# Sparse latent attention of a decoder layer: the second tile's logits in three fp32r passes, and the attention's output turned by VectorE alone

## The chip, the cores and the metric

One Trainium2 chip, one of its NeuronCores. The metric is the time of one execution on the device in microseconds. A core has TensorE (PE in the profile; PEld is its loading of stationary operands), VectorE (DVE), ScalarE (ACT), GpSimd (POOL) and SyncE (SP), which issues the DMAs here. The engines run their own lists of instructions and wait for each other on semaphores.

## The reference

One layer over 256 tokens of width 2048, in fp32. h = rmsnorm(x) is projected by one matrix; three token mixers read their columns; each mixer's output (256 x 1024) is gated by SiLU, projected to 2048 columns, scaled by a sigmoid gate and summed; one more projection, a norm and the residual follow. The mixer of the change is the third, cut to its core:

```python
def dsa_attention(q, ckv, iq, ik, iw, kv_norm_g, ik_norm_g, w_uv):
    q = q.reshape(b, s, 8, 256)                      # 8 heads, latent width 256
    c = rmsnorm(ckv, kv_norm_g)                      # 256 x 256, shared by the heads
    ...                                              # each query selects at most 64 keys
    logits = einsum('bqhc,bqkc->bqhk', q, c_sel) * 256 ** -0.5
    p = softmax(where(valid, logits, -inf))
    ob = einsum('bqhk,bqkc->bqhc', p, c_sel)
    return einsum('bqhc,hcv->bqhv', ob, w_uv)        # 8 heads x 128
...
y_c = dsa_attention(...) * silu(dsa_z)
mixed += sigmoid(gate_2) * (y_c @ w_branch[2])
```

## The kernel before

**Tiling.** The 256 tokens are two tiles of 128 partitions (TILES). All large products go through `multiply` (L1510): x (or y) is the stationary operand, split into a high part rounded to fp32r and the remainder (`xhi`/`xlo`, `yhi`/`ylo`); the weights are split the same way, and high x high, high x low and low x high are added in PSUM (L1526, L1527, L1528). Weights come in units of 256 rows by 512 columns (512 KB). For each unit SyncE loads `raw` (L392), ScalarE rounds it to `whi` (`round_unit`, L566), VectorE subtracts to `wlo` (`split_unit`, L894), and TensorE makes 12 matmuls of it, 2.72 us. The rings have 4 slots, and in step k the two engines prepare unit k + 4, once TensorE is through with unit k.

**Stages around the change.** Three loops follow each other, one for each mixer's output (parts PP[0], PP[1], PP[2], "branches" one to three). Each has 4 turns of 12 units: 8 units of the gate's projection (reads xhi, xlo), then 4 units of the branch's projection (reads yhi, ylo), and at the end of a turn VectorE gates the result and adds it to `mixed` (`gate_branch`, L1262: 4 instructions at L1268 and L1275). The order on each engine is written out by hand: the small work of the mixers is put between the units.

**Sparse attention** runs within the loop of PP[1]: two heads a turn, h = 2i + s, six steps (u) for each. `dsa_qT` holds q of one head turned, `cT` the latents turned; `chi` and `clo` are the split of `cT`, made earlier for another product.
- TensorE, u = 1: logits into M[1] (L1761 to 1765): columns 0:128 are tile 0 against keys 0:128, columns 128:384 tile 1 against all 256 keys, each as two fp32 matmuls over the latent width. u = 3: transposes of the probabilities (L1769). u = 4: times the values (L1777, L1779).
- VectorE, u = 1: mask (L1401) and maximum (L1404). u = 2: reciprocal of the sum and the SiLU gate (L1408 to 1411). u = 4: scale and gate the output into `area0` (L1418, `dsa_y`). u = 3 and 5: `turn_q` (L1323), 8 blocks each, turns q of the next head into `dsa_qT`; a block is one 32x32 STREAM_TRANSPOSE instruction over 128 elements (L885), and sixteen make a head.
- ScalarE, u = 2: exp (L809) and tanh for the gate (L813). u = 3: copies the transposes out (L817). Its loop over the turns is a hardware loop (L801).

**The output turned.** Branch three needs y turned and split in `yhi`/`ylo`, eight blocks of 128 columns in four pairs b. Before: pairs 0 and 1 (heads 0 to 3) are turned by VectorE with `turn_yc` (L1382), sixteen instructions of 32x256, four in each of the steps 0 to 3 of the first turn of PP[2], into `yc_T`; pairs 2 and 3 (heads 4 to 7) by eight transposes on TensorE after its first unit of that turn (L1806) into PSUM M[2] and M[3]. ScalarE rounds a pair with `round_y` (L787), VectorE subtracts with `split_y` (L1368). TensorE waits in `branch_units` (L1710) for the last `ylo` ahead of unit 8 of the turn. SyncE waits for the same `ylo` (L486) ahead of loading x again (1 MB), and the next turn's units are queued behind that.

Of the kernel before, what the change touches and what calls it, by code (L numbers as in the profile page):

```python
# [38 lines left out]
P = 128  # L39
D_MODEL = 2048  # L40
SEQ = 256
# [120 lines left out]
def build(nc, x, pre_norm_g, w_in, da_lambda, da_norm_g, ml_conv_w, ml_conv_b, ml_gate_b, ml_norm_g,  # L162
          dsa_kv_norm_g, dsa_ik_norm_g, dsa_w_uv, w_branch, w_out, post_norm_g, out):
    with ExitStack() as ctx:
# [17 lines left out]
        clo = sb("clo", [P, 2, SEQ], F32R)  # L182
        mixed = sb("mixed", [P, TILES, D_MODEL])
# [107 lines left out]
        yc_T = view(area0[:, 0, :], 2048, 4, SEQ)  # L291
# [68 lines left out]
        dsa_turned = sem("dsa_turned")  # L360
        dsa_logits, dsa_negmax, dsa_exp = sem("dsa_logits"), sem("dsa_negmax"), sem("dsa_exp")
# [3 lines left out]
        merged_turned, merged_psum, y_psum = sem("merged_turned"), sem("merged_psum"), sem("y_psum")  # L365
# [191 lines left out]
        def _(act):  # L557
# [243 lines left out]
            with act.Fori(0, PP[1].turns) as i:  # L801
                for v in range(PAIR_UNITS):
                    round_unit(PP[1], i, v)
                    s, u = v // 6, v % 6
                    h = i * 2 + s
                    if u == 2:
                        act.wait_ge(dsa_negmax, h * 2 + 2)
                        for t, a, n in ((0, 0, P), (1, P, 2 * P)):
                            nc.scalar.activation(dsa_s[:, a:a + n], dsa_s[:, a:a + n], ACT.Exp,  # L809
                                                 bias=dsa_negmax_c[:, t:t + 1], accum_out=dsa_sum_c[:, t:t + 1]  # L810
                                                 ).then_inc(dsa_exp, 1)
                        act.wait_ge(dsa_y, h * 2 + 1)
                        nc.scalar.activation(dsa_sig, area0[:, :, bass.ds(h * P + 3 * WIDTH, P)], ACT.Tanh,  # L813
                                             scale=0.5).then_inc(dsa_tz, 1)
# [17 lines left out]
            for i in range(PP[2].turns - 1):  # L832
                for v in range(PAIR_UNITS):
                    round_unit(PP[2], i, v)
                    if i == 0 and v == 0:
                        for b in range(2, 4):
                            act.wait_ge(y_psum, b - 1)
                            round_y(b, M[b][:, :].rearrange("p (k s) -> p k s", k=2))
                    if i == 0 and v == 4:
                        for b in range(2):  # L840
                            act.wait_ge(y_turned, 4 + b + 1)
                            round_y(b, yc_T[:, 2 * b:2 * b + 2, :])
                    if v == FULL_UNITS - 1:
                        gates(PP[2], i, 8)
# [34 lines left out]
        def _(dve):  # L879
# [501 lines left out]

            def turn_yc(n):  # L1382

                if n == 0:
                    dve.wait_ge(dsa_y, 1 + TILES * DSA_HEADS // 2)
                last = turn_block(yc_T.rearrange("p k (t s) -> p k t s", t=TILES),
                                  area0[:, :, 3 * WIDTH:3 * WIDTH + 512].rearrange("p t (k d) -> p k t d", d=P), n)
                if n == 15:
                    last.then_inc(y_turned, 2)

            for i in range(PP[1].turns):
                steps.enter(0, 2 * 4)
                for v in range(PAIR_UNITS):
# [3 lines left out]
                    if u in (3, 5) and h < DSA_HEADS - 1:  # L1397
                        turn_q(h + 1, range(8) if u == 3 else range(8, 16))
# [15 lines left out]
                    if u == 4:  # L1414

                        dve.wait_ge(dsa_out, h + 1)
                        for t in range(TILES):
                            nc.vector.scalar_tensor_tensor(area0[:, t, bass.ds(h * P + 3 * WIDTH, P)],  # L1418
                                                           M[3][:, t * P:(t + 1) * P], dsa_rsum_c[:, t:t + 1],
                                                           dsa_sig[:, t, :], ALU.mult, ALU.mult).then_inc(dsa_y, 1)  # L1420
                gate_branch(PP[1], i, 4)
# [13 lines left out]
            for i in range(PP[2].turns - 1):  # L1435
                for v in range(PAIR_UNITS):
                    split_unit(PP[2], i, v)
                    if i == 0 and v < 4:
                        for n in range(4):
                            turn_yc(4 * v + n)  # L1440
                    if i == 0 and v == 1:
                        for b in range(2, 4):
                            split_y(b, M[b][:, :].rearrange("p (k s) -> p k s", k=2), 8 + b - 1)
                    if i == 0 and v == 5:
                        for b in range(2):
                            split_y(b, yc_T[:, 2 * b:2 * b + 2, :], 10 + b + 1)
# [62 lines left out]
        def _(pe):  # L1509
# [240 lines left out]
            with pe.Fori(0, PP[1].turns) as i:  # L1750
                for v in range(PAIR_UNITS):
# [6 lines left out]
                    if u == 1:  # L1758
                        pe.wait_ge(ylo_ready, 9)
                        pe.wait_ge(dsa_turned, h + 1)  # L1760
                        for t, a, n in ((0, 0, P), (1, P, 2 * P)):  # L1761
                            for c in range(2):
                                last = nc.tensor.matmul(M[1][:, a:a + n], dsa_qT[:, c, t * P:(t + 1) * P],  # L1763
                                                        cT[:, c, 0:n], start=(c == 0), stop=(c == 1))
# [28 lines left out]
            def pair_turn(i, first):  # L1793

                for v in range(PAIR_UNITS):
# [4 lines left out]
                    if first and v == 0:  # L1800
                        pe.wait_ge(dsa_y, 1 + TILES * DSA_HEADS)
                        for b in range(2, 4):
                            for j in range(2):
                                for t in range(TILES):
                                    kt = 2 * b + j
                                    last = nc.tensor.transpose(M[b][:, j * SEQ + t * P:j * SEQ + (t + 1) * P],  # L1806
                                                               area0[:, t, 3 * WIDTH + kt * P:3 * WIDTH + (kt + 1) * P],
                                                               ident[:, :])
                            last.then_inc(y_psum, 1)

            pair_turn(0, True)
            with pe.Fori(1, PP[2].turns - 1) as i:
                pair_turn(i, False)
# [52 lines left out]
```

## Time and profile before

| | before |
|---|---|
| median of 3 runs | 1093.58 us (1093.2 to 1093.67) |
| profiled execution, its time | 1092.95 us |
| its span, first to last instruction | 1091.2 us |
| TensorE busy | 1080.8 us |
| VectorE busy | 810.7 us |
| ScalarE busy | 538.7 us |
| GpSimd busy | 15.0 us |
| mean granted TensorE clock | 0.998 |

How to read it: "busy" is the time in which at least one instruction of the engine was running. Matmuls overlap, a matmul of 512 columns is shown with some 0.39 us but one starts every 0.227 us, so prices on TensorE are read from starts. The time of an execution is 1.75 us more than its span here. In the timelines below a line is the start, the duration, the engine, the source line, the operation, output and input, shapes, the number of instructions merged, and in brackets the idle time of the engine before it with what ended it.

### The profile page before, as it was taken

To read this page: it belongs to the slowest core of one execution; us is meant where nothing else is said; L and a number is where in the kernel's file an instruction comes from. 1 tells how busy PE (TensorE), PEld (TensorE's weight loads), DVE (VectorE), ACT (ScalarE), POOL (GpSimd) and SP (SyncE) were. 2 spreads that over 40 slices of the span, in tenths; PEclk is the share of its full clock that TensorE was granted. 3 is DMA by queue.
4 is the path that set the end of the run, shared out by engine and by line. 5 is a ranking of instruction groups with operands and counts; after the bars stand their busy time and mean duration, and the time that the engine had idled before them with its cause. 6 is when DMAs were issued, how large, how long until landed. Compare 5 with 4: busy or idle time off the path is not lost.

```text
span 1091.2 us, 14577 instructions
## 1 busy us (share of the span) xinstructions
PE 1080.8 (99%) x5041; PEld 896.6 (82%) x5041; DVE 810.7 (74%) x1441; ACT 538.7 (49%) x751; POOL 15.0 (1%) x41
## 2 busy tenths in 40 slices
PE   9999999999999999999999999999999999999997
PEld 7898888888887888889887778888888888888886
DVE  5555566688877888888888777878788777777445
ACT  5664444555555565555446444454444444436442
POOL 0000000000000000000000000000000000000000
PEclk9999999999999999999999999999999999999999
DMA  8776666566656656657656555654655567765552
GB/s 283 200 220 193 193 193 193 175 186 177 192 174 176 181 163 190 196 160 229 207 161 190 175 170 174 213 175 141 196 171 163 153 219 259 229 196 182 194 194 109
DMA packets 114122, 205.83 MB, mean 189 GB/s; under 512 B 11229, under 2 KB 18457, under 8 KB 113689
## 3 DMA queue, kind: packets, MB, share of 16 engines
q1 hardware_dynamic: 114032, 205.21, 61.8%
q8 instruction: 25, 0.41, 0.1%
q14 instruction: 25, 0.20, 0.1%
q10 hardware_dynamic: 40, 0.01, 0.0%
HBM read 203.10 MB, written 2.10 MB: 188 GB/s over the span
## 4 chain that ended last, share of the span: by engine, by line
PE 92%; DVE 6%; ACT 1%; issue 0%; DMA 0%; DVEq 0%; ACTq 0%
PE stream L1526 29%; PE stream L1528 28%; PE stream L1527 28%; DVE wlo L894 2%; PE stream L1647 1%; PE mixer L1763 1%; DVE mixed L885 1%; DVE area L885 1%; ACT whi L566 1%; PE stream L1648 0%; PE mixer L1779 0%; PE mixer L1625 0%; PE mixer L1730 0%; PE mixer L1561 0%; PE mixer L1729 0%
## 5 line engine op out<-in xcount | busy, mean ns | idle before, releaser
L566 ACT ACTIVATE whi<-raw 128x1024 fp32r<-128x1024 f32 (+1 forms) x376 | 395.5, 1054 | 505.6 <-PE stream L1528 479.2
L894 DVE TENSOR_TENSOR wlo<-raw,whi 128x1024 fp32r<-128x1024 f32 (+1 forms) x376 | 456.4, 1217 | 243.0 <-ACT whi L566 239.6
L1526 PE MATMUL stream<-whi,xboth 128*128 128x512 f32 (+1 forms) x1248 | 490.4, 393 | 0.0
L1528 PE MATMUL stream<-whi,xboth 128*128 128x512 f32 (+1 forms) x1248 | 484.0, 388 | 0.0
L1527 PE MATMUL stream<-wlo,xboth 128*128 128x512 f32 (+1 forms) x1248 | 483.6, 387 | 0.0
L1526 PEld LDWEIGHTS stream<-whi,xboth 128*128 128x128 f32 x1248 | 234.5, 188 | 50.9 <-issue 4.9
L1528 PEld LDWEIGHTS stream<-whi,xboth 128*128 128x128 f32 x1248 | 234.4, 188 | 48.5
L1527 PEld LDWEIGHTS stream<-wlo,xboth 128*128 128x128 f32 x1248 | 234.6, 188 | 46.0
L1526 PE MATMUL stream<-whi,yhi 128*128 128x512 f32 x192 | 76.7, 399 | 0.3 <-DVE ylo L1368 0.3
L1528 PE MATMUL stream<-whi,ylo 128*128 128x512 f32 x192 | 75.0, 390 | 0.0
L1527 PE MATMUL stream<-wlo,yhi 128*128 128x512 f32 x192 | 74.8, 389 | 0.0
L885 DVE STREAM_TRANSPOSE mixed<-area 32x128 f32<-32x128 f32 x224 | 67.7, 302 | 3.7
L885 DVE STREAM_TRANSPOSE scratch<-area 32x128 f32<-32x128 f32 (+1 forms) x160 | 50.5, 316 | 2.8
L1526 PEld LDWEIGHTS stream<-whi,yhi 128*128 128x128 f32 x192 | 36.1, 188 | 8.4 <-issue 1.3
L1528 PEld LDWEIGHTS stream<-whi,ylo 128*128 128x128 f32 x192 | 36.0, 188 | 7.8
L1527 PEld LDWEIGHTS stream<-wlo,yhi 128*128 128x128 f32 x192 | 36.1, 188 | 7.3
L1647 PE MATMUL stream<-xboth,whi 128*128 128x384 f32 x120 | 35.1, 361 | 0.2 <-ACT area L573 0.2
L1648 PE MATMUL stream<-xboth,wlo 128*128 128x192 f32 x120 | 30.0, 250 | 0.0
L573 ACT ACTIVATE area<-stream,tiny 128x512 f32<-128x512 f32 (+1 forms) x44 | 27.6, 677 | 3.3 <-DVE mixed L885 2.9
L1647 PEld LDWEIGHTS stream<-xboth,whi 128*128 128x128 f32 x120 | 22.6, 188 | 0.6 <-issue 0.4
L1648 PEld LDWEIGHTS stream<-xboth,wlo 128*128 128x128 f32 x120 | 22.9, 191 | 0.1
L885 DVE STREAM_TRANSPOSE area<-mixed 32x256 f32<-32x256 f32 x48 | 20.9, 436 | 1.0
(241 smaller groups left out, 554.1 us busy)
## 6 DMA issues: line engine op xcount, KB each, us to landing
raw<-in_w_in SPq DMA_DIRECT2D x286, 512.0 KB, 3.6
raw<-in_w_branch SPq DMA_DIRECT2D x48, 512.0 KB, 4.6
raw<-in_w_out SPq DMA_DIRECT2D x32, 512.0 KB, 3.7
raw<-in_w_in SPq DMA_DIRECT2D x12, 256.0 KB, 3.2
mixed<-in_x SPq DMA_DIRECT2D x8, 256.0 KB, 6.5
area<-in_x SPq DMA_DIRECT2D x2, 1024.0 KB, 6.6
out<-area SPq DMA_DIRECT2D x8, 256.0 KB, 2.3
raw<-in_dsa_w_uv SPq DMA_DIRECT2D x4, 256.0 KB, 2.9
```

What stands on the lines that cost most here:

```text
L566: nc.scalar.activation(whi[:, slot, :, 0:width], raw[:, slot, :, 0:width], ACT.Copy).then_inc(whi_ready, 1)
L573: nc.scalar.activation(to[t], stream[bank_pair][t][:, 0:width], ACT.Copy, scale=rstdx[:, t:t + 1]).then_inc(banks_free, 1)
L885: return nc.vector.transpose(to[c * 32:(c + 1) * 32, :, :, p * 32:(p + 1) * 32], of[p * 32:(p + 1) * 32, :, :, c * 32:(c + 1) * 32])
L894: nc.vector.tensor_tensor(wlo[:, slot, :, 0:width], raw[:, slot, :, 0:width], whi[:, slot, :, 0:width].bitcast(F32), ALU.subtract).then_in ...
L1526: nc.tensor.matmul(to, left_hi[:, kt, tokens], high, start=first, stop=False)
L1527: nc.tensor.matmul(to, left_hi[:, kt, tokens], low, start=False, stop=False)
L1528: last = nc.tensor.matmul(to, left_lo[:, kt, tokens], high, start=False, stop=final)
L1647: nc.tensor.matmul(both_to, high, xboth[:, kt, :, TOPK:], start=kt == 0, stop=False)
L1648: last = nc.tensor.matmul(low_to, low, xhi[:, kt, TOPK:], start=False, stop=False)
L1763: last = nc.tensor.matmul(M[1][:, a:a + n], dsa_qT[:, c, t * P:(t + 1) * P], cT[:, c, 0:n], start=(c == 0), stop=(c == 1))
```

## The change

The part of tile 1 of the logits is computed in three fp32r passes. ScalarE rounds the turned q of tile 1 to `dsa_qhi`, VectorE makes the remainder `dsa_qlo` (`split_q`), and TensorE adds qhi x chi, qhi x clo and qlo x chi over both halves of the latent width, six matmuls of 256 columns in place of two fp32 ones. Tile 0 stays as it is. TensorE waits for `dsa_qlo` between the two. ScalarE's copy for the next head stands in its step u = 5 behind the rounding, and waits for the turned q; VectorE's subtraction in its step u = 5. The turns of q move from steps 3 and 5 (8 and 8) to steps 2, 3 and 4 (4, 6 and 6). ScalarE's loop over the turns is written out in the program.

The output is turned by VectorE alone. Heads 0 to 3 are turned (sixteen 32x256 instructions) in steps 1 to 5 of the last head (2, 3, 4, 3, 4), heads 4 to 7 in steps 0 to 3 of branch three's first turn, four each. The eight transposes on TensorE go, and its first turn of branch three joins the loop. `round_y` stands in steps 0 (pairs 0, 1) and 4 (pairs 2, 3), `split_y` in steps 1 and 5.

```diff
@@ -288,7 +290,7 @@
-        yc_T = view(area0[:, 0, :], 2048, 4, SEQ)
+        yc_T = [view(area0[:, c, :], 2048, 4, SEQ) for c in range(2)]
@@ -798,11 +801,18 @@
-            with act.Fori(0, PP[1].turns) as i:
+            act.wait_ge(dsa_turned, 1)
+            nc.scalar.activation(dsa_qhi[:, :, :], dsa_qT[:, :, P:], ACT.Copy).then_inc(dsa_qhi_ready, 1)
+
+            for i in range(PP[1].turns):
                 for v in range(PAIR_UNITS):
                     round_unit(PP[1], i, v)
                     s, u = v // 6, v % 6
                     h = i * 2 + s
+                    if u == 5 and h < DSA_HEADS - 1:
+                        act.wait_ge(dsa_logits, h + 1)
+                        act.wait_ge(dsa_turned, h + 2)
+                        nc.scalar.activation(dsa_qhi[:, :, :], dsa_qT[:, :, P:], ACT.Copy).then_inc(dsa_qhi_ready, 1)
@@ -832,14 +842,10 @@
-                    if i == 0 and v == 0:
-                        for b in range(2, 4):
-                            act.wait_ge(y_psum, b - 1)
-                            round_y(b, M[b][:, :].rearrange("p (k s) -> p k s", k=2))
-                    if i == 0 and v == 4:
-                        for b in range(2):
+                    if i == 0 and v in (0, 4):
+                        for b in range(v // 2, v // 2 + 2):
                             act.wait_ge(y_turned, 4 + b + 1)
-                            round_y(b, yc_T[:, 2 * b:2 * b + 2, :])
+                            round_y(b, yc_T[b // 2][:, 2 * (b % 2):2 * (b % 2) + 2, :])
@@ -1379,13 +1385,23 @@
+            def split_q(h):
+
+                dve.wait_ge(dsa_qhi_ready, h + 1)
+                nc.vector.tensor_tensor(dsa_qlo[:, :, :], dsa_qT[:, :, P:], dsa_qhi[:, :, :].bitcast(F32),
+                                        ALU.subtract).then_inc(dsa_qlo_ready, 1)
+
+            split_q(0)
+
             def turn_yc(n):
 
-                if n == 0:
-                    dve.wait_ge(dsa_y, 1 + TILES * DSA_HEADS // 2)
-                last = turn_block(yc_T.rearrange("p k (t s) -> p k t s", t=TILES),
-                                  area0[:, :, 3 * WIDTH:3 * WIDTH + 512].rearrange("p t (k d) -> p k t d", d=P), n)
-                if n == 15:
+                c = n // 16
+                if n % 16 == 0:
+                    dve.wait_ge(dsa_y, 1 + TILES * DSA_HEADS // 2 * (c + 1))
+                last = turn_block(yc_T[c].rearrange("p k (t s) -> p k t s", t=TILES),
+                                  area0[:, :, 3 * WIDTH + c * 512:3 * WIDTH + (c + 1) * 512].rearrange(
+                                      "p t (k d) -> p k t d", d=P), n % 16)
+                if n % 16 == 15:
                     last.then_inc(y_turned, 2)
@@ -1394,8 +1410,8 @@
-                    if u in (3, 5) and h < DSA_HEADS - 1:
-                        turn_q(h + 1, range(8) if u == 3 else range(8, 16))
+                    if u == 5 and h < DSA_HEADS - 1:
+                        split_q(h + 1)
@@ -1418,6 +1434,11 @@
+                    if u in (2, 3, 4) and h < DSA_HEADS - 1:
+                        turn_q(h + 1, {2: range(4), 3: range(4, 10), 4: range(10, 16)}[u])
+                    if 0 < u and h == DSA_HEADS - 1:
+                        for n in {1: range(2), 2: range(2, 5), 3: range(5, 9), 4: range(9, 12), 5: range(12, 16)}[u]:
+                            turn_yc(n)
@@ -1437,13 +1458,10 @@
                     if i == 0 and v < 4:
                         for n in range(4):
-                            turn_yc(4 * v + n)
-                    if i == 0 and v == 1:
-                        for b in range(2, 4):
-                            split_y(b, M[b][:, :].rearrange("p (k s) -> p k s", k=2), 8 + b - 1)
-                    if i == 0 and v == 5:
-                        for b in range(2):
-                            split_y(b, yc_T[:, 2 * b:2 * b + 2, :], 10 + b + 1)
+                            turn_yc(16 + 4 * v + n)
+                    if i == 0 and v in (1, 5):
+                        for b in range(v // 2, v // 2 + 2):
+                            split_y(b, yc_T[b // 2][:, 2 * (b % 2):2 * (b % 2) + 2, :], 8 + b + 1)
@@ -1758,10 +1776,15 @@
-                        for t, a, n in ((0, 0, P), (1, P, 2 * P)):
-                            for c in range(2):
-                                last = nc.tensor.matmul(M[1][:, a:a + n], dsa_qT[:, c, t * P:(t + 1) * P],
-                                                        cT[:, c, 0:n], start=(c == 0), stop=(c == 1))
+                        for c in range(2):
+                            nc.tensor.matmul(M[1][:, 0:P], dsa_qT[:, c, 0:P], cT[:, c, 0:P],
+                                             start=(c == 0), stop=(c == 1))
+                        pe.wait_ge(dsa_qlo_ready, h + 1)
+                        for c in range(2):
+                            to = M[1][:, P:3 * P]
+                            nc.tensor.matmul(to, dsa_qhi[:, c, :], chi[:, c, :], start=(c == 0), stop=False)
+                            nc.tensor.matmul(to, dsa_qhi[:, c, :], clo[:, c, :], start=False, stop=False)
+                            last = nc.tensor.matmul(to, dsa_qlo[:, c, :], chi[:, c, :], start=False, stop=(c == 1))
                         last.then_inc(dsa_logits, 1)
@@ -1790,27 +1813,16 @@
-            def pair_turn(i, first):
+            def pair_turn(i):
...
-                    if first and v == 0:
-                        pe.wait_ge(dsa_y, 1 + TILES * DSA_HEADS)
-                        for b in range(2, 4):
-                            for j in range(2):
-                                for t in range(TILES):
...
-                            last.then_inc(y_psum, 1)
...
-            pair_turn(0, True)
-            with pe.Fori(1, PP[2].turns - 1) as i:
-                pair_turn(i, False)
+
+            with pe.Fori(0, PP[2].turns - 1) as i:
+                pair_turn(i)
```

## Rows read from the trace of the kernel before

**Rows 1.** The page, part 1: busy time, share of the span, instructions.

```profile
PE 1080.8 (99%) x5041; PEld 896.6 (82%) x5041; DVE 810.7 (74%) x1441; ACT 538.7 (49%) x751; POOL 15.0 (1%) x41
```

**Rows 2.** Waits, 712 to 900 us: waiter, what it waited for, total, times, longest.

```profile
PE stream L1526 <- DVE ylo L1368: 0.3, 1, 0.3
```

**Rows 3.** The chain that ended last, 845 to 905 us: start, duration, engine, line.

```profile
850.64 1.31 PE mixer L1763 x8
...
864.02 1.07 ACT whi L566
...
866.26 1.28 DVE area L1268 x2
...
868.77 1.23 DVE wlo L894
...
881.62 0.45 DVE area L885
...
882.63 0.62 ACT yhi L787
...
884.23 1.23 DVE wlo L894
885.46 1.21 DVE ylo L1368 x2
...
886.91 0.47 PE stream L1526
```

**Rows 4.** Timeline of TensorE around the logits of head 1.

```profile
737.84 1.47 PE L1763 MATMUL mixer<-scratch 128*128 128x128 f32 x8
...
739.38 0.40 PE L1527 MATMUL stream<-wlo,yhi 128*128 128x512 f32 x1
```

**Rows 5.** Timeline of TensorE: the small projection, then the indexer's queries.

```profile
58.79 0.32 PE L1526 MATMUL stream<-whi,xboth 128*128 128x344 f32 x1
...
68.91 0.32 PE L1526 MATMUL stream<-whi,xboth 128*128 128x344 f32 x1
...
500.91 0.25 PE L1648 MATMUL stream<-xboth,wlo 128*128 128x192 f32 x1
...
501.20 0.25 PE L1648 MATMUL stream<-xboth,wlo 128*128 128x192 f32 x1
```

**Rows 6.** Timeline of VectorE: head 7, then the first turns of the output.

```profile
855.85 1.23 DVE L894 TENSOR_TENSOR wlo<-raw,whi 128x1024 fp32r<-128x1024 f32 x1 [1.74 <-ACT whi L566]
...
857.39 0.43 DVE L1411 SCALAR_TENSOR_TENSOR scratch<-scratch,area 128x256 f32<-128x256 f32 x1
858.65 1.23 DVE L894 TENSOR_TENSOR wlo<-raw,whi 128x1024 fp32r<-128x1024 f32 x1 [0.83 <-ACT whi L566]
861.67 1.23 DVE L894 TENSOR_TENSOR wlo<-raw,whi 128x1024 fp32r<-128x1024 f32 x1 [1.80 <-ACT whi L566]
...
865.11 1.23 DVE L894 TENSOR_TENSOR wlo<-raw,whi 128x1024 fp32r<-128x1024 f32 x1 [1.70 <-ACT whi L566]
...
869.92 1.77 DVE L885 STREAM_TRANSPOSE area<-area 32x256 f32<-32x256 f32 x4
```

**Rows 7.** Timeline of VectorE: head 0, a group of turns of q and the output's scaling.

```profile
728.39 2.50 DVE L885 STREAM_TRANSPOSE scratch<-area 32x128 f32<-32x128 f32 x8
...
732.05 0.60 DVE L1418 SCALAR_TENSOR_TENSOR area<-mixer,tiny,scratch 128x128 f32<-128x128 f32 x2
```

**Rows 8.** Timeline of TensorE: the output's transposes and the second matmul behind them.

```profile
866.55 1.04 PE L1806 MATMUL mixer<-ident,area 128*128 128x128 f32 x8
...
867.66 0.39 PE L1527 MATMUL stream<-wlo,xboth 128*128 128x512 f32 x1
```

**Rows 9.** Stretches at the end: stretch, length, busy (count) of PE, PEld, DVE, ACT, POOL; clock; DMA share, GB/s.

```profile
1084.00:1085.00 1.00, 0.20 (x1) 0.00 (x0) 0.05 (x1) 0.69 (x2) 0.00 (x0) 1.00 0.72 275
...
1087.00:1088.00 1.00, 0.00 (x0) 0.00 (x0) 1.00 (x3) 0.00 (x0) 0.00 (x0) 0.71 0.64 240
```

## Prediction: what the change does to the time

> **What bounds the kernel now.** I read four views in this order. First the page: TensorE is busy for 99% of the span and VectorE for 74% [rows 1], so the time is TensorE's list of work plus whatever it waits for. Then the waits of the stretch that the change touches (712 to 900 us): TensorE waits for another engine there once, 0.3 us, for `ylo` of L1368 [rows 2]. Then the chain that ended last, between 845 and 905 us. The reader is to see in it where it leaves TensorE: up to the rounding at 864.02 it is TensorE's stream, then it runs over VectorE (L1268 at 866.26, the split of unit 0 at 868.77, the turns of the output, the last at 881.62), ScalarE (`yhi`, 882.63), VectorE again (split of unit 5 at 884.23, `ylo` at 885.46), and TensorE's first product with y starts at 886.91 [rows 3]. So VectorE has no slack between about 866 and 887 us although it is idle a quarter of the whole time: the wait of 0.3 us is what is left of a race that TensorE nearly ties. What TensorE saves before 855 us shortens the kernel; what it saves between 866 and 887 us only lengthens that wait; what VectorE gets extra ahead of 882 us lengthens the kernel. Last, the timelines of TensorE and VectorE price the parts.
>
> **Logits of the second tile (L1761 to 1765), eight times.** The block of one head is eight records: each fp32 product is two records. It takes 1.31 us in the chain [rows 3]; in the timeline it begins at 737.84 and the stream's pitch is regained with the matmul at 739.38 [rows 4], (739.38 - 737.84) less one pitch of 0.227 = 1.31 again. Four records have 128 columns, four 256: by columns 1.31/12 = 0.109 for a short one, 0.218 for a long one. The short ones stay (0.44). The long ones (0.87) give way to six fp32r products of 256 columns. None of that width is in the trace. From the small projection, 344 columns: from 58.79 to 68.91 are 66 matmuls, 0.153 each [rows 5]; with 0.227 for 512 that is 0.44 ns a column, so 0.115 us at 256. The other bound is a pair of 384 and 192 columns, 501.20 - 500.91 = 0.29 for 576 columns [rows 5], 0.127 us at 256. I take 0.116, since equal passes in a row are like the small projection: 6 x 0.116 = 0.70. Saving per head 0.87 - 0.70 = 0.17 (bounds 0.11 and 0.18), times eight 1.4 us (0.9 to 1.5; if the additional wait in the middle of the block stops the look-ahead of the weights, it can fall to nothing, a rival below). It is all on the path, as all eight blocks come before 855 us, where the chain is TensorE's.
>
> The Trainium skill (TensorE: Matmul & The Clock Gate, Back-to-back issue gap) gives an isolated gap of the columns at 2.4 GHz plus some 2.5 ns. Here the 512 columns take 227 ns, some 11 ns more than that rule gives. By the rule a pass would be 0.109 and the eight heads would save 1.7 us, 0.3 more than my sum; the rows decide.
>
> **Feeding these products.** New per head: a copy to `dsa_qhi` on ScalarE (128x256, 0.4 us by the nearest row of that shape, L1411 of VectorE at 0.43 [rows 6]) and a subtraction on VectorE (same shape, 0.4). The wait for `dsa_turned` stands in ScalarE ahead of the next unit's rounding, the wait for `dsa_qhi` in VectorE ahead of the next split. The turns of q are spread anew: eight 32x128 turns take 2.50 us, 0.31 each [rows 7]; they now are 4, 6 and 6 in steps 2, 3 and 4, where they were 8 and 8 in steps 3 and 5. L1418 of head 0 is at 732.05 and takes 0.60 [rows 7]; it comes no later than now, as 10 turns and not 8 stand ahead but four of them in the idle time before step 3. Then six turns to 734.5; the split of step 5 (1.25) to 735.8, and the subtraction to 736.2. TensorE's next block starts at 737.84 [rows 4]: 1.6 us to spare, so these cost nothing. ScalarE's copy at 734.5 lies between the roundings. Once the cover of 1.6 us is gone each microsecond more costs one per head. Before the loop the pair for head 0 fits in the same way; ScalarE's loop written out turn by turn, and TensorE's first turn of branch three folded into the loop, I put at nothing: neither engine's issue is late in this stretch (ScalarE waits there for TensorE, the only wait of TensorE is the one above).
>
> **Eight transposes less on TensorE (L1806).** They begin at 866.55, and the pitch is regained at 867.66 [rows 8]: 1.11 less 0.23 is 0.88 us. That lies after 866 us, where VectorE is the chain. So TensorE comes 0.88 us earlier to the wait for `ylo` and waits 0.88 longer: worth nothing. That is the main difference between the work saved and the time saved.
>
> **Sixteen turns more on VectorE, in the last head.** Four turns of 32x256 in branch three take 1.77 with a pitch of 1.79 to the next [rows 6], 0.447 each. The change puts sixteen of them, 7.15 us, into steps 1 to 5 of head 7 (2, 3, 4, 3, 4). Head 7 has no turns of q in either kernel, so they fall into idle time first: 1.74 before the split at 855.85, 0.83 before 858.65, then 1.80 and 1.70 [rows 6]. I follow the engine. Step 1: two turns end by 855.0, before the split of step 2 can start: free. Step 2: split at 855.85, L1411 at 857.39 to 857.85, three turns to 859.19. Step 3: split 1.25, four turns 1.80, to 862.24. Step 4: split 1.15, L1418 0.62, three turns 1.34, to 865.35. Step 5: split 1.25, four turns 1.80, to 868.40. The gating (L1268, L1275) takes 868.77 - 866.26 = 2.51 [rows 3], to 870.91. Before, the next split started at 868.77 [rows 3]. So VectorE enters branch three 2.14 us late, with no idle time left in which to catch up: the four steps with turns (c = 1) and the two `ylo` of the first half in step 1 are the same work as now. The 32 turns thus end at 884.2, not 882.06, and the tail from there (ScalarE's `yhi`, the rounding of unit 5, VectorE's split and two `ylo`) takes the same 4.8 us: TensorE's product with y starts at 889.05 on the clock of before. The extra 2.14 (bounds 1.8 and 2.6: a split takes 1.23 [rows 6] and lets its follower start after 1.15 to 1.25, the first of the turns after 869.92 - 868.77 = 1.15 [rows 3, 6]) is on the path in full. No unit is late meanwhile: the closest is unit 8's split, done 885.4 where TensorE wants it at 885.6.
>
> **After the wait** everything is tied to `ylo` in both kernels: ScalarE's next roundings, the DMA queue (x again and the next turn's units are queued behind the same wait), and VectorE's next splits. So the shift stays as it is to the end.
>
> **Sum.** -1.4 (logits) + 2.14 (turns) + 0 (transposes) = +0.75 us. The profiled execution took 1092.95 (span 1091.2), which would become 1093.7 (span 1092.0). The median of the runs shown is 1093.58, 0.63 above it: 1094.3.
>
> **Rivals.**
> (1) The clock falls in the gap. TensorE's idle time before its first product with y grows from 0.28 to 0.28 + 0.88 + 2.14 = 3.3 us. At the end of the span TensorE's last work ends at 1084.2, and the granted clock is down in the stretch from 1087 on, 0.71 in that microsecond, which puts the fall at 1087.4, 3.2 us after the last matmul [rows 9]. The gap is as long as that, a coin's throw against its phase; against it speaks that there the idleness had no end. Each microsecond at the low level (1.2 GHz) loses half a microsecond. How soon it rises again no row shows; taken as the 3.2 us that it took to fall, 1.6 us is lost, up to 3 if it takes twice that: 1095.9 (to 1097.3). This ends on the slow side, and decides from a gap of about 3 us. The skill (same page, HAM oscillation — how this bites in real kernels) says that a TensorE left without work in gaps is put back to the low clock and has to earn the high one anew; the trace agrees for its one long gap, the end, and this rule speaks against the change.
> (2) The three passes save nothing, as the additional wait in the middle keeps the next weights from being loaded ahead, or they run at the price of 0.145 each: +2.14, 1095.7. For it: six instructions of 0.12 us in place of four of 0.22; against it: the waits that stand ahead of such blocks now show no gap [rows 4].
> (3) The turns are hidden after all, because some of VectorE's idle time that I count as used stays: then the wait for `ylo` doesn't grow but goes. -1.4 - 0.88 - 0.28 = -2.6, 1091.0. Against it: the chain runs over VectorE there now [rows 3], and 7.15 us go into about 5 that can be used.
> (4) The subtraction for `dsa_qlo` comes later than 1.6 us more than worked out, and TensorE waits in each head; at 0.5 us a head +4 on top: 1098.
>
> **How the numbers follow.** Forecast 0.60, (1) 0.18, (2) 0.10, (3) 0.08, (4) 0.04. Most likely 1094.3. The range takes in the forecast with its bounds (0.9 to 1.5 saved, 1.8 to 2.6 added: 1093.9 to 1095.3, and half a microsecond for the median), (2) and most of (1): 1092.6 to 1096.9. 0.2%, about what a measurement of this kernel can tell from no change, is 2.2 us. Faster is (3), 0.08. Slower is most of (1), part of (2) and (4), 0.22. Within is the rest, 0.70.
>
> **What would show it.** Right: L1763's successor at some 1.14 us a block; TensorE's wait for `ylo` 3.2 to 3.5 us and still its only one in the stretch; no VectorE idle time from 856 to 884; the gating of head 7's turn 2.1 us later against TensorE's stream. Wrong: a wait for `dsa_qlo`; a granted clock under 1.00 near 890 us; a wait for `ylo` under 1 us.

## The result

The changed kernel took 1095.08 us (median of 15 executions, 1093.79 to 1097.03), the kernel before 1093.24 (15 executions, 1092.55 to 1093.67): ratio 1.0023, 95% interval 1.0016 to 1.0030. That is 1.84 us more by the medians, whose own ratio is 1.0017 and lies within the interval. The forecast was 1094.3 within 1092.6 to 1096.9.

The executions of the changed kernel don't lie around one value. Each has a mean granted clock of its span: three have 0.998, as in the profiled execution of before, and took 1093.79, 1093.97 and 1094.34; six have 0.996 or 0.997 and took 1094.83 to 1095.09; six have 0.995 and took 1096.53 to 1097.03. The profiled one is of the last kind (1096.83, span 1095.1).

The waits from 712 to 900 us, where before there was only [rows 2] for TensorE (waiter, what it waited for: total, times, longest):

```profile
ACT dsa_qhi L815 <- DVE scratch L891: 6.7, 7, 1.0
PE stream L1544 <- DVE ylo L1374: 3.4, 1, 3.4
```

ScalarE waits for the turned q at most 1.0 us a head, which stays hidden. TensorE still waits for another engine once, for `ylo`, but 3.4 us and not 0.3. No wait for `dsa_qlo` has appeared. The timeline of VectorE from head 7 on answers to [rows 6]:

```profile
854.93 1.23 DVE L900 TENSOR_TENSOR wlo<-raw,whi 128x1024 fp32r<-128x1024 f32 x1 [0.78 <-ACT whi L569]
...
858.27 1.22 DVE L900 TENSOR_TENSOR wlo<-raw,whi 128x1024 fp32r<-128x1024 f32 x1
...
861.32 1.22 DVE L900 TENSOR_TENSOR wlo<-raw,whi 128x1024 fp32r<-128x1024 f32 x1
...
864.45 1.23 DVE L900 TENSOR_TENSOR wlo<-raw,whi 128x1024 fp32r<-128x1024 f32 x1
865.70 1.80 DVE L891 STREAM_TRANSPOSE area<-area 32x256 f32<-32x256 f32 x4
867.53 1.29 DVE L1274 SCALAR_TENSOR_TENSOR area<-area,stream 128x512 f32<-128x512 f32 x2
...
870.05 1.22 DVE L900 TENSOR_TENSOR wlo<-raw,whi 128x1024 fp32r<-128x1024 f32 x1
...
883.37 1.22 DVE L900 TENSOR_TENSOR wlo<-raw,whi 128x1024 fp32r<-128x1024 f32 x1
885.50 1.22 DVE L900 TENSOR_TENSOR wlo<-raw,whi 128x1024 fp32r<-128x1024 f32 x1 [0.91 <-ACT whi L569]
886.65 1.28 DVE L1374 TENSOR_TENSOR ylo<-area,yhi 128x512 fp32r<-128x512 f32 x2
```

After the split at 854.93 the brackets are gone: the idle times of 0.83, 1.80 and 1.70 us in [rows 6] are filled, and VectorE works without a break to 884.6. TensorE at the wait and behind it:

```profile
884.36 0.39 PE L1546 MATMUL stream<-whi,xboth 128*128 128x512 f32 x1
888.17 0.79 PE L1544 MATMUL stream<-whi,yhi 128*128 128x512 f32 x1 [3.43 <-DVE ylo L1374]
...
889.19 0.63 PE L1546 MATMUL stream<-whi,ylo 128*128 128x512 f32 x1
889.62 0.63 PE L1544 MATMUL stream<-whi,yhi 128*128 128x512 f32 x1
...
893.82 0.40 PE L1545 MATMUL stream<-wlo,yhi 128*128 128x512 f32 x1
894.06 0.39 PE L1546 MATMUL stream<-whi,ylo 128*128 128x512 f32 x1
```

Two things are to be seen. The product with y starts after 3.43 us without work, and then a matmul starts every 0.43 us and not every 0.23, until 893.5. The stretches say why (start and end, length, busy time and count of PE, PEld, DVE, ACT, POOL, granted clock, DMA share, GB/s):

```profile
884.00:886.00 2.00, 0.74 (x4) 0.28 (x2) 1.09 (x2) 2.00 (x4) 0.00 (x0) 1.00 0.18 70
886.00:888.00 2.00, 0.00 (x0) 0.00 (x0) 2.00 (x4) 2.00 (x4) 0.00 (x0) 0.73 0.00 0
888.00:890.00 2.00, 1.82 (x4) 1.49 (x5) 2.00 (x2) 0.52 (x1) 0.00 (x0) 0.50 0.41 82
890.00:892.00 2.00, 2.00 (x6) 1.57 (x5) 0.20 (x1) 0.00 (x0) 0.00 (x0) 0.50 0.97 399
892.00:894.00 2.00, 2.00 (x6) 1.57 (x6) 0.00 (x0) 0.00 (x0) 0.00 (x0) 0.57 1.00 384
894.00:896.00 2.00, 2.00 (x10) 1.63 (x10) 0.54 (x1) 1.06 (x1) 0.00 (x0) 1.00 1.04 399
```

The granted clock falls to 0.50 (1.2 GHz) within the idle stretch, at about 886.9 us, and is back at 2.4 GHz at about 893.7. From 888.17 to there are 5.6 us at the low level. What they cost is seen in the rest of the span, which is the same work in both kernels: from the first product with y to the last instruction there are 1091.2 - 886.91 = 304.3 us before and 1095.1 - 888.17 = 306.9 changed, so 2.6 us are lost. The Trainium skill (TensorE: Matmul & The Clock Gate, HAM oscillation — how this bites in real kernels) tells of a TensorE that waits in gaps between its work, is put back to the low clock and starts again at it. This trace agrees, with these rows.

**Where the time went.** The spans differ by 3.9 us. To separate the parts I take the time from the first block of logits, before which the two programs differ in nothing that takes time on TensorE, to the first product with y. It leaves out the 0.5 us by which executions differ at the very start. The first block starts here in the kernel before and in the changed one (timelines of TensorE):

```profile
719.08 1.47 PE L1763 MATMUL mixer<-scratch 128*128 128x128 f32 x8
```

```profile
719.55 0.60 PE L1780 MATMUL mixer<-scratch 128*128 128x128 f32 x4
719.91 0.36 PE L1785 MATMUL mixer<-chi,dsa_qhi 128*128 128x256 f32 x1
720.11 0.28 PE L1786 MATMUL mixer<-clo,dsa_qhi 128*128 128x256 f32 x1
720.23 0.28 PE L1787 MATMUL mixer<-chi,dsa_qlo 128*128 128x256 f32 x1
...
720.70 0.40 PE L1544 MATMUL stream<-whi,xboth 128*128 128x512 f32 x1
720.94 0.40 PE L1545 MATMUL stream<-wlo,xboth 128*128 128x512 f32 x1
```

Before, the product with y starts at 886.91 [rows 3], 167.83 us after 719.08. Changed, it is 888.17 - 719.55 = 168.62: 0.79 us more, where the sum of the prediction says 0.75. The rest of the 3.9 us is the start (0.47) and the low clock (2.6): 0.79 + 0.47 + 2.6 = 3.9.

### The profile page after: what moved, and what is told of

It is laid out like the page before. It is cut to its first block, busy times and chain, and to the rows that moved or that the text cites. A ratio compares the mean times of both kernels' runs of the same rounds, so it can differ in the third digit from the quotient of the medians.

```text
span 1095.1 us, 14580 instructions
## 1 busy us (share of the span) xinstructions
PE 1081.4 (99%) x5049; PEld 897.5 (82%) x5049; DVE 820.8 (75%) x1465; ACT 541.4 (49%) x759; POOL 15.0 (1%) x41
## 4 chain that ended last, share of the span: by engine, by line
PE 91%; DVE 7%; ACT 1%; issue 1%; DMA 0%; DVEq 0%; ACTq 0%
PE stream L1544 29%; PE stream L1546 28%; PE stream L1545 28%; DVE wlo L900 3%; DVE area L891 1%; PE stream L1665 1%; DVE mixed L891 1%; ACT whi L569 1%; PE stream L1666 0%; PE mixer L1643 0%; PE mixer L1780 0%; PE mixer L1748 0%; PE mixer L1579 0%; PE mixer L1747 0%; PE mixer L1802 0%
## 5 line engine op out<-in xcount | busy, mean ns | idle before, releaser
L891 DVE STREAM_TRANSPOSE area<-area 32x256 f32<-32x256 f32 x48 | 20.9, 436 | 1.0
```

Source lines behind the costliest of these rows:

```text
L891: return nc.vector.transpose(to[c * 32:(c + 1) * 32, :, :, p * 32:(p + 1) * 32], of[p * 32:(p + 1) * 32, :, :, c * 32:(c + 1) * 32])
```

## The experiments

In the table "way" is the time from the first block of logits to the first product with y, from the profiled execution of each kernel; "wait" is TensorE's wait for `ylo` there; the ratio is to the kernel before on the same chip.

| kernel | way, us | wait, us | median, us | ratio, 95% interval |
|---|---|---|---|---|
| before | 167.83 | 0.28 | 1093.24 | |
| changed | 168.62 | 3.43 | 1095.08 | 1.0023 (1.0016 to 1.0030) |
| logits_only | 166.42 | 0.30 | 1091.22 | 0.9986 (0.9977 to 0.9995) |
| turns_only | 169.98 | 3.37 | 1097.04 | 1.0038 (1.0025 to 1.0052) |
| before_late2 | 169.99 | 2.42 | 1096.80 | 1.0033 (1.0022 to 1.0043) |
| warm20 | 168.67 | 1.28 | 1093.88 | 1.0007 (0.9998 to 1.0016) |
| warm10 | 168.66 | 2.37 | 1094.07 | 1.0012 (1.0003 to 1.0021) |
| first_half_early | 165.96 | none | 1090.54 | 0.9982 (0.9973 to 0.9991) |
| spread | 166.64 | 1.22 | 1091.57 | 0.9989 (0.9980 to 0.9998) |
| spread_ylo4 | 165.29 | none | 1090.45 | 0.9978 (0.9969 to 0.9987) |

**One part alone: the logits.** The changed kernel, with the output's part put back:

```diff
-                    if 0 < u and h == DSA_HEADS - 1:
-                        for n in {1: range(2), 2: range(2, 5), 3: range(5, 9), 4: range(9, 12), 5: range(12, 16)}[u]:
-                            turn_yc(n)
...
-                            turn_yc(16 + 4 * v + n)
+                            turn_yc(4 * v + n)
...
+                    if first and v == 0:
+                        pe.wait_ge(dsa_y, 1 + TILES * DSA_HEADS)
...
```

> The kernel before with the logits' part of the change alone (three passes, the split of q, the turns of q moved); the output is turned as before. Theory (the eight shorter blocks are on the path, as they lie ahead of the stretch where VectorE is the chain): 1.4 us less than before, 1091.8 against 1093.2; TensorE's wait for ylo stays at about 0.3 us, no clock under 1.00 near 890 us. Rival (the six passes with the additional wait cost as much as the four long records): no change, 1093.2.

The way is 1.41 us shorter, the wait stays at 0.30, the clock at 1.00. The median is 1.95 less than that of before on its chip (1093.17), with an interval of 0.5 to 2.5 that holds the 1.4. The three passes bring what they were said to, and that part alone makes the kernel faster.

**The other part alone: the output.** The kernel before with the output's part of the change, logits as they were:

```diff
-                        for c in range(2):
-                            nc.tensor.matmul(M[1][:, 0:P], dsa_qT[:, c, 0:P], cT[:, c, 0:P],
-                                             start=(c == 0), stop=(c == 1))
-                        pe.wait_ge(dsa_qlo_ready, h + 1)
...
+                        for t, a, n in ((0, 0, P), (1, P, 2 * P)):
+                            for c in range(2):
...
```

> The kernel before with the output's part alone (all turns on VectorE, sixteen in head 7); logits as before. Theory: VectorE enters branch three 2.1 us late, TensorE's product with y starts 2.1 us later and its wait grows to 3.3 us: 1095.4 where the clock holds, and up to 2.5 us more (1097.9) in runs in which it falls in that gap, so several levels of time within one kernel. Rival (the two parts only cost when together, since the split of q on VectorE makes the lateness): under 1094.

The way is 2.15 us longer, the wait 3.37. So the two parts add: -1.41 + 2.15 = +0.74, against +0.79 for both. The lateness of VectorE is due to the turns and not to the split of q. The median is up by 3.87, more than 2.15, and the profiled execution shows the rest; these are its matmuls after the wait:

```profile
889.25 0.49 PE L1534 MATMUL stream<-whi,yhi 128*128 128x512 f32 x1 [3.37 <-DVE ylo L1367]
889.58 0.49 PE L1535 MATMUL stream<-wlo,yhi 128*128 128x512 f32 x1
889.87 0.63 PE L1536 MATMUL stream<-whi,ylo 128*128 128x512 f32 x1
890.30 0.63 PE L1534 MATMUL stream<-whi,yhi 128*128 128x512 f32 x1
...
892.86 0.53 PE L1534 MATMUL stream<-whi,yhi 128*128 128x512 f32 x1
893.23 0.39 PE L1535 MATMUL stream<-wlo,yhi 128*128 128x512 f32 x1
```

Here the clock falls when TensorE has already been at work again for half a microsecond (0.43 us from start to start only from 889.87 on; the granted clock of the stretch from 888 to 890 is 0.93, which puts the fall at 889.7). In the stretch from 892 to 894 it is 0.71, so it is back at 893.2: low for 3.4 us, which costs 1.7 (from the first product with y to the end there are 306.0 us in place of 304.3), and 2.15 + 1.7 = 3.85. The 1095.4 that was expected where the clock holds can't be seen: all five executions have a mean clock of 0.995 to 0.997.

**Fill the gap.** The changed kernel, with 20 (then 10) transposes of the identity on TensorE between its last work ahead of the wait and the wait:

```diff
+                    if first and v == FULL_UNITS - 1:
+                        for _ in range(20):
+                            nc.tensor.transpose(M[2][:, 0:P], ident[:, :], ident[:, :])
```

> The changed kernel with 20 transposes of the identity on TensorE (0.11 us each, 2.1 us) into a free bank right ahead of the wait for ylo in branch three's first turn: they fill the gap, and leave about 1.3 us of it. Theory (the spread of the changed kernel's times, 1093.8 to 1097.0, is the clock falling in the gap): the clock stays at 1.00 there, all runs lie within 1093.3 to 1094.4, median 1094.0, although TensorE does more. Rival (the spread comes from the loads queued behind the same wait): levels and median stay as they are, 1095.1, or rise by the work added.

TensorE does 2 us more work and the kernel is 1.2 us faster than the changed one (1.1 us, where each is compared with the kernel before on its own chip: +0.71 and +1.84). The way is the same (168.67 against 168.62), as the wait shrinks by what the transposes take. The spread is gone: eleven executions within 1093.31 to 1094.46, against 1093.79 to 1097.03. So the difference between the forecast's 0.75 and the measured 1.84 us, and the levels, are the clock's.

> The changed kernel with 10 transposes of the identity in the gap ahead of the wait for ylo, half of what warm20 had: some 2.3 us of the gap are left. Theory (only the length of TensorE's idle stretch and its phase decide whether the clock falls, as in before_late2, where 2.4 us was enough in most runs): some runs fall and some don't, two levels about 1.7 us apart, 1093.8 and 1095.5. Rival (what matters is that TensorE was idle for over 3 us, and the levels of before_late2 come from something else): one level as with warm20, 1093.9.

The theory's first half came out and its distance did not. Eight executions have a mean clock of 0.998 and took 1093.87 to 1094.42; three have 0.996 or 0.997 and took 1094.87 to 1095.00, some 0.9 us more and not 1.7. So the single level of the rival is not there. Why the three lose only 0.9 us stays open, as none of them was profiled. The profiled execution is one of the eight and keeps its clock over a gap of 2.37 us:

```profile
886.00:888.40 2.40, 0.03 (x2) 0.04 (x1) 2.40 (x4) 2.40 (x4) 0.00 (x0) 1.00 0.01 3
888.40:892.00 3.60, 3.60 (x16) 3.00 (x17) 2.01 (x2) 0.31 (x1) 0.00 (x0) 1.00 0.77 257
```

So a gap of 2.4 us keeps the clock in most executions of this kernel and loses it in some. The next kernel has a gap of the same length and loses it in most. The length by itself doesn't settle it.

**The lateness by itself.** The kernel before, with seven additional turns on VectorE:

```diff
+                    if i == 0 and v in (2, 3):
+                        for n in range(4 if v == 2 else 3):
+                            turn_block(view(area1[:, 1, :], 3 * WIDTH, 4, SEQ).rearrange("p k (t s) -> p k t s", t=TILES),
+                                       area0[:, :, 3 * WIDTH:3 * WIDTH + 512].rearrange("p t (k d) -> p k t d", d=P),
+                                       4 * v + n)
```

> The kernel before with seven additional 32x256 turns on VectorE in steps 2 and 3 of branch three's first turn, written to an area that nobody reads (3.1 us more on VectorE, none of the change). Theory: it passes one to one to TensorE's product with y, the wait for ylo grows from 0.3 to 3.4 us and the kernel by 3.1 us, 1096.3 where the clock holds and up to 2.5 more where it falls. Rival (VectorE has slack there, and the changed kernel's lateness comes from elsewhere): less than 1.5 us more, under 1094.8.

The way grows by 2.16 us and not by 3.1, the wait to 2.42. The timeline of VectorE shows where the remainder went:

```profile
877.52 3.57 DVE L885 STREAM_TRANSPOSE area<-area 32x256 f32<-32x256 f32 x8
881.10 1.23 DVE L894 TENSOR_TENSOR wlo<-raw,whi 128x1024 fp32r<-128x1024 f32 x1
882.36 3.17 DVE L885 STREAM_TRANSPOSE area<-area 32x256 f32<-32x256 f32 x7
885.54 2.36 DVE L894 TENSOR_TENSOR wlo<-raw,whi 128x1024 fp32r<-128x1024 f32 x2
887.82 1.29 DVE L1368 TENSOR_TENSOR ylo<-area,yhi 128x512 fp32r<-128x512 f32 x2
```

I had put the last three behind the real turns, whose last releases ScalarE. ScalarE rounds meanwhile, and VectorE's splits of units 8 and 9 now stand without the pause of 0.9 us between them that it otherwise spends waiting for ScalarE. Four of the seven (1.79) pass in full, the other three (1.34) less that 0.9: 2.2, as measured. The theory's one to one holds only ahead of the last turn. The kernel does nothing of the change, but it has the gap, and its times lie in two groups, 1094.34 and 1094.57 with a mean clock of 0.998, and six from 1096.64 to 1097.10 with 0.996 or 0.997. The profiled one, in the upper group:

```profile
888.00:889.60 1.60, 0.23 (x1) 0.26 (x2) 1.60 (x3) 1.33 (x3) 0.00 (x0) 1.00 0.00 0
889.60:890.60 1.00, 1.00 (x4) 0.81 (x4) 1.00 (x2) 0.00 (x0) 0.00 (x0) 0.65 0.63 90
890.60:893.00 2.40, 2.40 (x7) 1.83 (x7) 0.78 (x1) 0.00 (x0) 0.00 (x0) 0.50 0.84 338
```

Its gap lies from 886.95 to 889.37, and the clock falls at 889.9. That of warm10 lies a microsecond earlier, 886.0 to 888.4, and the clock stays. The place of the gap in time differs between these two; that the place decides is not shown, since nothing here moves it alone.

**Less on VectorE in branch three.** The changed kernel with the second half of the output on TensorE again, and the first half in head 7 as changed, so that VectorE enters branch three as late as in the changed kernel but has no turns there:

```diff
-                    if i == 0 and v < 4:
-                        for n in range(4):
-                            turn_yc(16 + 4 * v + n)
-                    if i == 0 and v in (1, 5):
-                        for b in range(v // 2, v // 2 + 2):
+                    if i == 0 and v == 1:
+                        for b in range(4):
...
```

> The changed kernel with the second half of the output turned on TensorE again (eight transposes, 0.88 us), the first half on VectorE in head 7 as changed; all of yhi and ylo in steps 0 and 1 of branch three. VectorE still enters branch three 2.1 us late. Theory (being late there costs only through ylo, which now is ready about 10 us before TensorE wants it): the wait for ylo is gone, the transposes are on the path, so it is logits_only less its wait of 0.3 us: 1090.9, one level of the clock. Rival (VectorE's lateness also delays wlo of the units, or the loads behind ylo): 1092 or more with a wait for wlo.

The wait is gone, with no wait for `wlo` in its place, the way is 165.96, 1.87 less than before (1.7 expected). The 0.2 more is the wait itself, which the profile shows as 0.28 but which costs more by the starts. In the kernel before:

```profile
886.25 0.39 PE L1528 MATMUL stream<-whi,xboth 128*128 128x512 f32 x1
886.91 0.47 PE L1526 MATMUL stream<-whi,yhi 128*128 128x512 f32 x1 [0.28 <-DVE ylo L1368]
```

From start to start these are 0.66 us and not the usual 0.23, so the wait costs 0.43. Being late in branch three costs nothing as such: it cost through `ylo` alone. And the transposes, 0.88 us on TensorE's path, are a fair price: the kernel is faster than both.

**The same turns, spread.** The changed kernel with the first half's turns spread from the end of head 4 on, where their input has long been there:

```diff
-                    if 0 < u and h == DSA_HEADS - 1:
-                        for n in {1: range(2), 2: range(2, 5), 3: range(5, 9), 4: range(9, 12), 5: range(12, 16)}[u]:
+                    if h >= DSA_HEADS // 2:
+                        for n in YC_AT.get((h, u), ()):
...
+            YC_AT = {(4, 5): range(2), (5, 0): range(2, 3), (5, 5): range(3, 5), (6, 0): range(5, 6),
+                     (6, 5): range(6, 8), (7, 0): range(8, 9), (7, 1): range(9, 11), (7, 2): range(11, 12),
+                     (7, 3): range(12, 14), (7, 4): range(14, 16)}
```

> The changed kernel with the sixteen turns of the first half spread over the idle time of heads 4 to 7 (2, 3, 3 and 8 of them) and none in step 5 of head 7; all else as changed. Theory (the sixteen turns cost because they are packed into one head): VectorE enters branch three on time, ylo comes at the same place as in the kernel before, the wait is 1.2 us (0.3 and the 0.88 of the transposes), no fall of the clock: 1091.3, as logits_only, that is 3.8 us less than the changed kernel. Rival (any sixteen turns more delay ylo, or delay wlo or the split of q in earlier heads): 1093 or more.

Measured 1091.57, 3.5 us less than the changed kernel, and a wait of 1.22, the clock held in the profiled execution, times within 1091.19 to 1092.09. The way is 1.98 us shorter than the changed kernel's, with all of its work still there, and VectorE's first split of branch three starts 148.51 us after the first block of logits (867.91 - 719.40), where the changed kernel has 150.50. So it isn't the sixteen turns but where they stand that cost the 2 us, and with them the clock. Spreading them isn't quite free either. In head 6 ScalarE's exp waits for the maximum, and TensorE, ahead of the transposes of the probabilities, for the exp, which it does in no other head and not in the changed kernel:

```profile
ACT scratch L819 <- DVE tiny L1424: 0.5, 1, 0.5
PEld mixer L1796 <- ACT scratch L819: 0.4, 1, 0.4
```

From the first block of logits to the first matmul of branch three there are 143.49 us here and 143.27 in the changed kernel: 0.2 us lost.

> As spread, and the two ylo of the first half move from step 1 of branch three's first turn, where they stand ahead of eight turns, to step 4 behind all the turns and ahead of the split of unit 9, with those of the second half right behind them. Theory (the chain turns, yhi, rounding of unit 5, split, ylo loses 1.2 us of VectorE ahead of it and 2.2 us of roundings and split inside it): ylo is ready before TensorE wants it, the wait is gone, and the 0.88 us of the transposes is gained at last: 1090.1. Rival (the split of unit 9 or the loads queued behind ylo become the bound): 1091 or more, with a wait for wlo.

```diff
-                    if i == 0 and v in (1, 5):
-                        for b in range(v // 2, v // 2 + 2):
+                    if i == 0 and v == 4:
+                        for b in range(4):
                             split_y(b, yc_T[b // 2][:, 2 * (b % 2):2 * (b % 2) + 2, :], 8 + b + 1)
```

VectorE in this kernel, and TensorE where it had waited:

```profile
878.54 1.79 DVE L891 STREAM_TRANSPOSE area<-area 32x256 f32<-32x256 f32 x4
880.36 1.22 DVE L900 TENSOR_TENSOR wlo<-raw,whi 128x1024 fp32r<-128x1024 f32 x1
881.50 2.49 DVE L1374 TENSOR_TENSOR ylo<-area,yhi 128x512 fp32r<-128x512 f32 x4
883.91 3.66 DVE L900 TENSOR_TENSOR wlo<-raw,whi 128x1024 fp32r<-128x1024 f32 x3
```

```profile
884.77 0.39 PE L1550 MATMUL stream<-whi,xboth 128*128 128x512 f32 x1
885.00 0.39 PE L1548 MATMUL stream<-whi,yhi 128*128 128x512 f32 x1
```

`ylo` is complete at 884.0 and TensorE goes from 884.77 to 885.00 without a pause. The way is 165.29, 2.54 us less than before, where 1.4 + 0.88 + 0.28 = 2.56 was expected. That the sum is met so closely is luck, as its parts differ: up to the first matmul of branch three the way is 1.21 us shorter (143.53 against 144.74; the two waits of spread stand in head 6 here too), and from there to the first product with y it is 1.33 shorter, 0.43 for the wait and 0.90 for the transposes. Only here do the transposes taken from TensorE shorten anything. With 1090.45 us it is the fastest of all, 2.4 us under before (0.9978, 0.9969 to 0.9987), though first_half_early at 1090.54 can't be told from it.

## Why the prediction was right

**Where the chain runs** was read rightly from [rows 3]: TensorE's stream to 864 us, VectorE from there to 887. before_late2 shows that additional work on VectorE ahead of the last turn lengthens the kernel, logits_only that work taken from TensorE ahead of it shortens it. That the shift stays as it is behind the wait holds too: from the first product with y to the end there are 304.2 to 304.3 us in every profiled execution that kept its clock.

**The logits**: the block takes 720.94 - 719.55 less one pitch of 0.227, 1.16 us (foretold 1.14), in place of 1.31; a pass starts every 0.12 (0.116 taken). Saved 1.41 on the way against 1.4. Eight times the 0.15 of the blocks is only 1.2, though. The remaining 0.2 us lie outside of the blocks, in time that the sum didn't price, and what shortened it is open; the sum came out as well as it did with some luck. One bound is worked out a little wrong as well: 0.29 us for 576 columns are 0.129 at 256 columns and not 0.127, so the saving's lower bound is 0.8 us and not 0.9. Nothing rests on it. The rule of the Trainium skill (TensorE: Matmul & The Clock Gate, Back-to-back issue gap) would have the pass at 0.109; the measured 0.12 decides. The wait in the middle costs nothing that shows but a pass of 0.20 in place of 0.12 to the second one, which the four short records' overlap gives back. Rival 2 falls.

**The split of q** is hidden, as said: no wait for `dsa_qlo`, and rival 4 falls.

**The turns**: VectorE's first split in branch three starts at 870.05, or 150.50 us after the first block of logits, before at 868.77 - 719.08 = 149.69: 0.81 later, which with the 1.4 saved ahead of it is 2.2 of lateness (2.14 foretold). Rival 3 falls. turns_only has 2.15 of it without the logits. **The transposes** were worth nothing in this kernel, and 0.90 in spread_ylo4. The loops written anew, put at nothing, show nowhere: the two parts alone add up to the whole within 0.05 us.

**The clock** is where the forecast's likeliest case was not the one that most executions show. The gap was foretold as 3.3 us and is 3.43. That the clock may fall in it was rival 1, with a chance of 0.18 and a price of 1.6 to 3 us; it fell, to judge by the mean clock and the times, in twelve of fifteen executions, and costs 2.6 us in the profiled one. A granted clock under 1.00 near 890 us was also named as a sign of being wrong, and it is there. The three in which it held took 1093.97 in their middle, 0.73 more than before: that is the forecast's case, although three executions that differ by 0.55 us can't confirm it to the tenth. The step that failed is the weighing in rival 1, "against it speaks that there the idleness had no end". I took [rows 9] as the time that it takes until the clock falls, when the row shows only one occurrence: in the changed kernel it fell 2.2 us after TensorE's last matmul and not 3.2, and in turns_only and before_late2 only after TensorE had gone back to work. The price of 1.6 to 3 us holds for the upper group, where the low clock lasted 6.8 us; the middle group lies only 1.0 us above the lowest and under that price. The direction and the range hold, the size does not: 1.84 us were measured where 0.75 was the sum, and 1.1 of it is the clock. The forecast of 1094.3 looks closer than that because it started from 1093.58, the median of three runs of the kernel before, where fifteen give 1093.24.

## What to carry to other kernels

When the chain that ended last leaves the busiest engine for a while, price what a change does to the engine that it runs over; work saved on the busiest engine there turns into waiting. Idle time of a helper engine can be used, but only up to the point where it is next in the chain: the same sixteen instructions cost 2 us packed into the last head and 0.2 spread over four. And a gap on TensorE of more than 2 us should be priced with the clock that it can cost: here that was 1.1 us in the median and 2.6 in the profiled execution, beside the 2.15 of the turns themselves.

## What the runs showed of the hardware

- By the mean clock of each execution, the granted clock fell for gaps of 3.4 us in 12 of 15 executions (changed) and 5 of 5 (turns_only), and for gaps of 2.4 us in 6 of 8 (before_late2) and 3 of 11 (warm10). It never showed with gaps of 1.2 to 1.3 us (spread, warm20, 22 executions).
- It can fall after the gap: 0.5 us after TensorE's return in turns_only (889.25, 889.7) and in before_late2 (889.37, 889.9).
- It stayed low for 3.4 us in these two and for 6.8 us in the changed kernel, where it fell 2.2 us after TensorE's last matmul ended.
- Twenty transposes of the identity on TensorE, ahead of a wait and into an idle bank, made the kernel 1.2 us faster. They shortened the gap from 3.43 to 1.28 us.
